# Retention's order of work: each head rotated right behind its projection, the three small-weight projections and their mixing moved in between the last heads

## The reference

```
p_rw, p_ret, p_hg, p_gate = split_sizes(h @ w_in[l], ...)
y_rw  = rwkv7_mixer(p_rw, ...)      # 8 heads of 64; small columns: decay, a and gate, 128 each
y_ret = retention_mixer(p_ret, ...) # 4 heads of 128
y_hg  = hgrn2_mixer(p_hg, ...)      # 4 heads of 128

def retention_mixer(p, pos, decay_param, n_ctx):
    q, k, v, g = split_sizes(p, (BRANCH_W,) * 4)
    q_h, k_h = rope(heads(q, H), pos), rope(heads(k, H), pos) * HEAD_DIM_RET ** -0.5
    # scores q k^T times gamma^|lag|, both directions, prefix rule for the context; times v
    return merge_heads(rms_norm(o)) * silu(g)
```

## Time and profile before

| | |
|---|---|
| median of 3 runs | 2376.91 us (2373.87 to 2386.03) |
| the profiled execution | 2386.95 us, span 2385.1 us |
| PE busy | 2180.2 us, 91% of the span |
| DVE busy | 1350.5 us, 57% |
| ACT busy | 971.2 us, 41% |
| POOL busy | 370.6 us, 16% |
| granted TensorE clock, mean | 0.960 of full |

### The profile page before, as it was taken

How to read it: one execution, slowest core, us unless ns; L and a number is a source line. 1 busy time by engine, 2 the same in 40 slices (tenths; PEclk the granted TensorE clock), 3 DMA queues, 4 the chain that set the end, 5 groups by cost and what they waited for, 6 DMA issues and landing times. The chain is left out here.

```text
span 2385.1 us, 50237 instructions
## 1 busy us (share of the span) xinstructions
PE 2180.2 (91%) x21268; PEld 1843.5 (77%) x21268; DVE 1350.5 (57%) x1956; ACT 971.2 (41%) x1385; POOL 370.6 (16%) x347
## 2 busy tenths in 40 slices
PE   7888999899999999999999998788888988998998
PEld 3555777778788688878888877577777877898998
DVE  5436575665466534464444456566666555567666
ACT  4534333232454232342322437434343454345544
POOL 0002221412234200000000000132233155100000
PEclk9998999999999999999999999899999989898999
DMA  7531412314211123322222232200000122355553
GB/s 284 193 124 58 152 66 106 134 55 152 72 62 58 67 97 101 136 81 97 98 97 97 97 144 94 85 12 28 20 12 29 38 71 67 112 185 182 175 182 125
DMA packets 64734, 241.32 MB, mean 101 GB/s; under 512 B 7296, under 2 KB 8448, under 8 KB 63104
## 3 DMA queue, kind: packets, MB, share of 16 engines
q1 hardware_dynamic: 62064, 218.66, 26.8%
q10 hardware_dynamic: 2448, 19.46, 2.1%
HBM read 231.80 MB, written 6.29 MB: 100 GB/s over the span
## 5 line engine op out<-in xcount | busy, mean ns | idle before, releaser
L397 PE MATMUL psum<-normed_high,weights_high 128*128 128x512 f32 (+1 forms) x1552 | 569.4, 367 | 19.7 <-DVE weight_ring_parts L1031 17.0
L1031 DVE TENSOR_TENSOR weight_ring_parts<-weight_ring,weights_high 128x1024 fp32r<-128x1024 f32 (+1 forms) x327 | 417.0, 1275 | 263.8 <-ACT weights_high L1544 256.5
L398 PE MATMUL psum<-normed_low_part,weights_high 128*128 128x512 f32 (+1 forms) x1552 | 555.9, 358 | 0.0
L399 PE MATMUL psum<-normed_high,weight_ring_parts 128*128 128x512 f32 (+1 forms) x1552 | 554.2, 357 | 0.0
L1544 ACT ACTIVATE weights_high<-weight_ring 128x1024 fp32r<-128x1024 f32 (+1 forms) x327 | 340.0, 1040 | 188.2 <-PE psum L399 136.7
L397 PEld LDWEIGHTS psum<-normed_high,weights_high 128*128 128x128 f32 x1552 | 306.7, 198 | 76.7 <-DVE weight_ring_parts L1031 27.7
L398 PEld LDWEIGHTS psum<-normed_low_part,weights_high 128*128 128x128 f32 x1552 | 306.2, 197 | 39.9 <-issue 2.0
L399 PEld LDWEIGHTS psum<-normed_high,weight_ring_parts 128*128 128x128 f32 x1552 | 305.1, 197 | 40.7
L470 PE MATMUL psum<-work 64*64 64x64 f32 (+1 forms) x7040 | 245.4, 225 | 33.0 <-issue 10.9
L470 PEld LDWEIGHTS psum<-work 64*64 64x64 f32 x7040 | 234.6, 136 | 51.8 <-issue 38.6
L397 PE MATMUL psum<-hidden_high,weights_high 128*128 128x512 f32 (+1 forms) x512 | 172.4, 337 | 3.7 <-DVE hidden_low L1486 3.7
(11 more groups left out here) (249 smaller groups left out, 3479.1 us busy)
## 6 DMA issues: line engine op xcount, KB each, us to landing
weight_ring<-in_weights SPq DMA_DIRECT2D x407, 512.0 KB, 3.5
x_scratch<-work ACTq DMA_DIRECT2D x2, 2048.0 KB, 11.7
weight_ring<-in_weights SPq DMA_DIRECT2D x16, 256.0 KB, 2.6
work<-x_scratch ACTq DMA_DIRECT2D x2, 2048.0 KB, 9.2
work<-in_ret_constants ACTq DMA_DIRECT2D x2, 1152.0 KB, 16.1
work<-in_x ACTq DMA_DIRECT2D x1, 2048.0 KB, 10.9
work<-in_small_weights ACTq DMA_DIRECT2D x1, 1152.0 KB, 6.6
constants<-in_constants ACTq DMA_DIRECT2D x1, 1024.0 KB, 8.9
```

Source lines behind the costliest of these rows:

```text
L397: mm(ps, w[0][:, cols], x[0], start=first, stop=False)
L398: mm(ps, w[0][:, cols], x[1], start=False, stop=False)
L399: return mm(ps, w[1][:, cols], x[0], start=False, stop=last)
L1031: tt(ring_r[:, i % RING, o], ring[:, i % RING, o], high[:, n % HIGHS, o].bitcast(F32), ALU.subtract).then_inc(vec_split.sem, vec_split.ste ...
```

## The change

1. `ret_order` is new. R(c) stands before A(c), right behind P(c), for all heads; before, R(c) stood behind A(c-1) and N(c-2). Three new steps S1, S2, S0 stand between the last heads' steps. In them PE projects small tile 1, 2 and 0.
2. The DMA order of the small tiles is 1, 2, 0 (and 3), to match. PSUM banks are named by hand (`small_bank`; N always takes bank 1).
3. ACT: in S2 it issues the DMA of the up matrices, waits for POOL's `pads` and does `raw` of tile 1; in S0 raw of tile 2; raw of tile 0 comes after "ret y" of head 3. The high weight parts are asked for at other places.
4. DVE: `mix` of tile 1 follows N2, of tile 2 follows O3, of tile 0 follows N3. Ahead of the last, `weights_low` makes the low parts up to the first RWKV key tile.
5. POOL: `pads` in S2, once the scores of head 3 are out of PSUM; `neighbours` where DVE mixes.

```diff
+MIXED_AT = {("N", 2): 1, ("O", 3): 2, ("N", 3): 0}
-    out += [("small", l, j) for j in range(3 if l == 0 else 4)]
+    out += [("small", l, j) for j in ((1, 2, 0) if l == 0 else (1, 2, 0, 3))]
-        ret_order = [("P", 0), ("R", 0), ("P", 1), ("A", 0), ("R", 1), ("O", 0), ("P", 2), ("A", 1), ("N", 0), ("R", 2),
-                     ("O", 1), ("P", 3), ("A", 2), ("N", 1), ("R", 3), ("O", 2), ("A", 3), ("N", 2), ("O", 3), ("N", 3)]
+        ret_order = [("P", 0), ("R", 0), ("P", 1), ("R", 1), ("A", 0), ("O", 0), ("P", 2), ("R", 2), ("A", 1), ("N", 0),
+                     ("O", 1), ("P", 3), ("R", 3), ("A", 2), ("S", 1), ("N", 1), ("O", 2), ("A", 3), ("S", 2), ("N", 2),
+                     ("O", 3), ("S", 0), ("N", 3)]
+        small_bank = {1: 2, 2: 3, 0: 0, 3: 2}
...
# PE
+                    if what == "S":
+                        big.start_at(small_bank[c])
+                        project(big, big_filled, split("small", l, c), ("small", l, c), lo if c == 2 else 0)
                     if what == "N":
                         eng.wait_ge(pool_ret.sem, pool_ret.at("ret squared", l, c))
+                        dense.start_at(1)
                         tile_sum(wk(RT_O + 512)[:, lo:N], ("rN", l, c), w)
-                big.start_at(3 * l)
-                for j in range(3 if l == 0 else 4):
-                    project(big, big_filled, split("small", l, j), ("small", l, j), lo if j == 2 else 0)
+                if l > 0:
+                    big.start_at(small_bank[3])
+                    project(big, big_filled, split("small", l, 3), ("small", l, 3))
+                big.start_at(3)
...
# DVE
+                        if c == 2:
+                            weights_low(split_at["small", l, 0] + 1)
...
-                eng.wait_ge(x_saved.sem, x_saved.at("x saved", l))
-                eng.wait_ge(loaded_masks.sem, loaded_masks.at("masks"))
-                weights_low(split_at["small", l, 2] + 1)
-                for j in range(3):
-                    mix(12 + j, wk(RW_SMALL + 512 * j), ("mixed", l, 12 + j))
-                    weights_low(min(split_at["small", l, j] + HIGHS, split_at["rw", l, 0, 2]) + 1)
...
+                    if (what, c) in MIXED_AT:
+                        j = MIXED_AT[what, c]
+                        if j == 1:
+                            eng.wait_ge(loaded_masks.sem, loaded_masks.at("masks"))
+                        if j == 0:
+                            weights_low(split_at["rw", l, 0, 1] + 1)
+                            eng.wait_ge(x_saved.sem, x_saved.at("x saved", l))
+                        mix(12 + j, wk(RW_SMALL + 512 * j), ("mixed", l, 12 + j))
+                weights_low(split_at["rw", l, 0, 2] + 1)
...
# ACT
-                        weights_high(split_at["ret", l, c, 2] + (HIGHS - 1 if l == 0 else HIGHS + 1))
+                        weights_high(split_at["ret", l, c, 2] + (HIGHS if c == 3 else HIGHS - 1) if l == 0 else split_at["ret", l, c, 2] + HIGHS + 1)
+                    if (what, c) == ("S", 2):
+                        eng.wait_ge(vec_ret.sem, vec_ret.at("roped", l, 3))
+                        n = 1536 if l == 0 else 2304
+                        eng.dma_start(wk(RW_W, n), wsm[l][:, 0:n]).then_inc(...)
+                        eng.wait_ge(pool_rwkv.sem, pool_rwkv.at("pads rwkv", l, -1))
+                        small_raw(1)
+                    if (what, c) == ("S", 0):
+                        small_raw(2)
+                        weights_high(split_at["rw", l, 0, 1] + 1)
                 eng.wait_ge(vec_ret.sem, vec_ret.at("ret y", l, 3))
...
+                small_raw(0)
+                weights_high(split_at["rw", l, 0, 2] + 1)
                 tables(SIGMOID)
-                for j in range(3):
-                    eng.wait_ge(big_filled.sem, big_filled.at("small", l, j))
-                    raw(12 + j, wk(RW_SMALL + 512 * j), big.get("small", l, j), ("drained", "small", l, j))
-                    weights_high(min(split_at["small", l, j] + HIGHS, split_at["rw", l, 0, 2]) + 1)
...
# POOL
+                    if (what, c) == ("S", 2):
+                        eng.wait_ge(vec_ret.sem, vec_ret.at("drained", "rA", l, 3, 2))
+                        eng.wait_ge(loaded_masks.sem, loaded_masks.at("masks"))
+                        pads(-1)
+                    if (what, c) in MIXED_AT:
+                        neighbours(12 + MIXED_AT[what, c])
-                eng.wait_ge(vec_ret.sem, vec_ret.at("ret y", l, 3))
-                eng.wait_ge(loaded_masks.sem, loaded_masks.at("masks"))
-                pads(-1)
-                for j in range(3):
-                    neighbours(12 + j)
```

More of the change, by code:

```diff
@@ L1108, in _, with mix @@
                 weights_low(split_at["ret", l, 0, 1] + 1)
+                def mix(i, dst, key):
+                    eng.wait_ge(act_rwkv.sem, act_rwkv.at("raw", l, i))
+                    raw = RW_SCR
+                    ctx = wants_context(l, i)
+                    grid = wk(raw + 258, 396).rearrange("p (r t) -> p r t", t=66)
+                    sides = wk(raw + 1166, NC)
+                    tt(sides.rearrange("p (r t) -> p r t", t=GRID), grid[:, 1:5, 0:64], grid[:, 1:5, 2:66], ALU.add).then_inc(
+                        vec_rwkv.sem, vec_rwkv.step())
+                    eng.wait_ge(vec_rwkv.sem, vec_rwkv.n)
+                    eng.wait_ge(act_rwkv.sem, act_rwkv.at("own part", l, i))
+                    stt(dst[:, NC:N], sides, dcol(D_QMU + i), dst[:, NC:N], ALU.mult, ALU.add).then_inc(vec_rwkv.sem, vec_rwkv.step())
+                    eng.wait_ge(vec_rwkv.sem, vec_rwkv.n)
+                    eng.wait_ge(pool_rwkv.sem, pool_rwkv.at("neighbours", l, i))
+                    if ctx:
+                        stt(dst[:, 0:NC], wk(raw + 654, NC), dcol(D_HMU + i), dst[:, 0:NC], ALU.mult, ALU.add).then_inc(vec_rwkv.sem, vec_rwkv.step())
+                        eng.wait_ge(vec_rwkv.sem, vec_rwkv.n)
+                    stt(dst[:, NC:N], wk(raw + 654 + NC, NC), dcol(D_QMU + i), dst[:, NC:N], ALU.mult, ALU.add).then_inc(vec_rwkv.sem, vec_rwkv.step(key))
+                    eng.wait_ge(vec_rwkv.sem, vec_rwkv.n)
                 for what, c in ret_order:
@@ L1179, in _ @@
                         eng.wait_ge(vec_ret.sem, vec_ret.n)
[L1182 to L1200, removed]
@@ L1640, in _, with raw, small_raw @@
                     eng.wait_ge(act_ret.sem, act_ret.n)
+                def raw(i, dst, ps, key):
+                    if last_mixed[0] is not None:
+                        eng.wait_ge(vec_rwkv.sem, vec_rwkv.at("mixed", l, last_mixed[0]))
+                    t0 = 0 if wants_context(l, i) else lo
+                    latent = ps[:, NC - t0:N - t0].rearrange("p (r t) -> p r t", t=GRID)
+                    grid = wk(RW_SCR + 258, 396).rearrange("p (r t) -> p r t", t=66)[:, 1:5, 1:65]
+                    if wants_context(l, i):
+                        act(wk(RW_SCR + 1, NC), ps[:, 0:NC], ACT.Copy).then_inc(act_rwkv.sem, act_rwkv.step())
+                        eng.wait_ge(act_rwkv.sem, act_rwkv.n)
+                    act(grid, latent, ACT.Copy).then_inc(act_rwkv.sem, act_rwkv.step(("raw", l, i)))
+                    eng.wait_ge(act_rwkv.sem, act_rwkv.n)
+                    act(dst[:, t0:N], ps[:, 0:N - t0], ACT.Copy, scale=dcol(D_OMU + i)).then_inc(act_rwkv.sem, act_rwkv.step(key))
+                    eng.wait_ge(act_rwkv.sem, act_rwkv.n)
+                    act_rwkv.also(("own part", l, i))
+                    last_mixed[0] = i
+                last_mixed = [None]
+                def small_raw(j):
+                    eng.wait_ge(big_filled.sem, big_filled.at("small", l, j))
+                    raw(12 + j, wk(RW_SMALL + 512 * j), big.get("small", l, j), ("drained", "small", l, j))
                 for what, c in ret_order:
@@ L1705, in _ @@
[L1705 to L1711 removed]
+                    if (what, c) == ("S", 2):
+                        eng.wait_ge(vec_ret.sem, vec_ret.at("roped", l, 3))
+                        n = 1536 if l == 0 else 2304
+                        eng.dma_start(wk(RW_W, n), wsm[l][:, 0:n]).then_inc(loaded_small_weights.sem, loaded_small_weights.step(("small weights", l), 16))
+                        eng.wait_ge(pool_rwkv.sem, pool_rwkv.at("pads rwkv", l, -1))
+                        small_raw(1)
@@ L1715, in _ @@
                     eng.wait_ge(act_rwkv.sem, act_rwkv.n)
-                    weights_high(min(split_at["small", l, 3] + HIGHS, split_at["rw", l, 0, 2]) + 1)
                 eng.wait_ge(vec_rwkv.sem, vec_rwkv.at("mixed", l, 12))
@@ L1966, in _ @@
                 lo, w, m0 = first_query(l)
-                for what, c in ret_order:
-                    if what == "O":
-                        eng.wait_ge(vec_ret.sem, vec_ret.at("drained", "rO", l, c))
-                        if c > 0:
-                            eng.wait_ge(dense_filled.sem, dense_filled.at("rN", l, c - 1))
```

(2 more changed lines are left out.)

11 lines of the change are left out of this document (8 added, 3 removed).

## The result

| | before | changed |
|---|---|---|
| median (20 runs each) | 2378.22 us (2373.87 to 2386.03) | 2389.47 us (2379.19 to 2395.58) |
| ratio of the times | | 1.0033, 95% interval 1.0022 to 1.0044 |
| the profiled execution | 2386.95 us, span 2385.1 | 2382.81 us, span 2381.0 |
| PE busy; granted clock | 2180.2 us; 0.960 | 2160.1 us; 0.964 |

The account below looks back on a forecast made before the run. PE was taken to bound the kernel, idling at waits for DVE around the last heads. Layer 0's -0.6 and layer 1's +8.8 us gave +8.2 on the median 2376.91, so 2385 us, range 2374 to 2396.

Parts of the forecast that it names:

- Part 1: Layer 0, head 1's rotation ahead of head 0's scores: strips pushed back, PE waits 9.1 us; +8.3 us.
- the upper bound of the term: Layer 0, head 1's rotation moved ahead: 10.5 us if PE's clock stays at its low level into head 2's projections.
- Part 2: Layer 1, head 1's rotation waits for ACT's query copy and holds back the strips; PE waits about 23 us; +20.4 us.
- Part 3: Rotations of heads 2 and 3 moved ahead: shorter waits -2.2, no restart -2.8 in layer 0; -2.5, clock -1.0 in layer 1.
- Part 4: Last heads up to the low-rank matmuls, small projections in between: -3.9 us in layer 0, -8.1 in layer 1.
- the bound given for a held clock: Layer 1, last heads to the low-rank matmuls: -10.6 us if no clock loss follows the new wait.
- The sum: Whole kernel: layer 0 -0.6 and layer 1 +8.8, together +8.2 us, +0.34%.
- the second rival: Last heads: moved mixing becomes the new wait, layer 1 slack 0.3 us; the 12.0 us gain fails, 2397 at worst; chance 0.16.
- The rival of the interleaving: Head 0's delay is hidden, so the later gains remain: 2356 us, or 2371 with half of it; chance 0.06.
- The clock rival: PE's clock falls in two short waits before the last heads (+5) or holds at the end (-5): 2380 to 2390; chance 0.16.
- its second case: PE keeps its clock over the two 3.3 us waits at the end, one per layer: -5 us.

Follow-up runs that it names:

- head 1 put back: Changed kernel with only head 1's rotation returned to its old place behind head 0's scores; 2359.83 us, 0.9915 of the time before.
- strips first: Changed kernel, but DVE builds the decay strips ahead of head 1's rotation, both still ahead of head 0's score copies; 2378.68 us, 0.999 of before.
- rotations only: Kernel before with the rotations of heads 1, 2 and 3 moved right behind their projections, no small-tile steps; 2378.99 us, 1.0000.
- rotations 2 and 3: Kernel before with only the rotations of heads 2 and 3 moved right behind their projections; 2355.40 us, 0.9901; again 2353.90 us, 0.9904.

## Why the prediction was right

**What bounds it.** Right: all that moved lies in the stages around the waits that the timeline of PE named, and the strips were the place where it lost.

**Part 1** (+8.3, bounds 6.3 to 10.5): +8.7 to +10.6 by the stages (38.9 and 38.6 against 28.3 to 29.9). The wait is 9.84 where 9.1 was said; DVE took the 6.85 us block first, as worked out. The step that was mis-sized is the clock: PE stayed at its lower level (granted clock 0.50) through O0 up to P2's first matmul, so that O0 took 5.49 us against 2.85, 2.6 more where 1.3 was charged. That is the case of the upper bound of the term. With R1 put back the stage is 9.1 us shorter.

**Part 2** (+20.4, bounds 18 to 22): +20.5 to +21.6; PE waits 23.29 us (said: about 23), DVE 13.20 for ACT (said: 13), and O0 starts 47.7 us after the layer's first projection instead of 27.3, the 20.4 that were worked out. One step was not right: the clock was held to be at its lower level at O0 already, "so no more is lost", yet O0 took 3.78 us behind the long wait against 2.92 before, 0.9 more. The mechanism was tested by itself: taking the strips out from behind the wait gave 11 us back and no more.

**Part 3** (-2.2 -2.8 in layer 0, -2.5 -1.0 in layer 1): A1-A2 is 3.8 to 5.1 us shorter in layer 0 and 4.1 to 4.8 in layer 1. Right; PE's clock held over the new waits of 1.6 and 2.3 us, as assumed.

**Part 4** (-3.9, -8.1): -3.6 to -3.8 and -11.4 to -11.6. Layer 1 gained some 3.4 us more than said, beyond the bound given for a held clock. Up to N3 the sum was right within 1.5 us (N3 at +21.6 of the stage against 22.6, the low part at +25.5 against 26.3), and behind the wait of 3.32 us I had charged 2.5 for the clock, which in both profiles of the changed kernel held. With head 1 put back and with the strips first it fell, and there the stage is 38.2 and 38.3. What was wrong in meaning, though not in sum, is whose gain it was: part 4 was told as that of the interleaving, and "rotations only", with no S step, has the same gain (6.9 and 9.2 us off the two stages, 16.1 together against 15.4 here): it is R3's. In the stages the S steps are neutral. In the runs they are not clearly so: with them the kernel is slower by 0.33% beside "rotations only" and by 0.37 and 0.39% by themselves, more than the stages hold; between "head 1 put back" (0.9915) and "rotations 2 and 3" (0.9901) the intervals overlap. The cause is open.

**The sum.** +8.2 said; the stages give +5.4 to +7.5, the ratio 7.9 (5.2 to 10.5). Of the terms, parts 1 and 2 came out up to 3.5 us too low together, part 3 was right within 1.3 in each layer, and part 4 some 3.4 us too small a gain: errors of opposite sign, of which a few us cancelled by luck, but none as large as the terms themselves.

**The rivals.** The end gave what it should, the strips cost what they should. The slack of the second rival was in fact used up in layer 1: ACT's raw of tile 1 ends at 1519.47, N2's sum at 1519.42, as these rows of the changed kernel show.

```profile
1518.78 0.69 ACT L1665 ACTIVATE work<-psum,derived 128x512 f32<-128x512 f32 x1
```

```profile
1518.82 0.60 PE L467 MATMUL psum<-work,constants 128*128 128x256 f32 x2
```

No wait of PE came of it, since O3 and S0 stood behind the sum. The rival of the interleaving (0.06) is refuted where it counts. The Trainium skill, Perfetto Trace Analysis, section Optimization Strategy, says that interleaving regimes with different contended engines may improve a kernel. This case does not show such a gain: the interleaved small projections brought none in the stages, and the rotation moved to where it waits for another engine cost 20 us in layer 1. The clock rival had the right reason: what the clock does behind a wait of 2 to 3.5 us differs between executions. Half of its second case came true: the clock held over the wait behind N3 in layer 1 and fell over the one in layer 0, in both profiles. It was sized for the changed stages alone; most of the scatter (9 us) arises elsewhere. Last, the prediction held that a change under 0.5% can't be told from none; with twenty runs of each kernel the interval lies clear of 1.

## What to carry to other kernels

When a step is moved ahead in an engine's fixed order, ask not only whether its own inputs are ready but what stands behind it: here a rotation that waits 13 us for a copy held back a strip build that needed nothing, and the engine that bounds the kernel stood still for 23 us, once per layer, which ate all of a 1% gain. Move each step of a repeated pattern by itself: heads 2 and 3 gained, head 1 alone lost, since the first round holds one-time work that the others don't have. And try the small part alone: two moved entries of a list did as much as the whole change without its flaw.

## What was not expected of the hardware

The granted clock after an idle time of 2 to 3.5 us is not a property of the kernel alone, nor of the length of the wait. The same wait of 2.96 us in front of the same 171 matmuls was followed by 23.4 us or 20.8 us, and a wait of 2.22 us in front of the same eight by 3.75 or 1.97. Over the last third of the kernel before, such places together made 845.6 against 836.4 us. Stage by stage the profiles repeat within 0.1 us where the clock does the same in all (17.6 or 17.7 us for A1-A2 in layer 1, in nine profiles of six kernels), so for a change of 0.3% the stages tell more than the end of one execution, and the end of many runs more than both where two kernels differ in what follows.
